# A hybrid decoder layer: blocks of L stored whole and read by a strided load, substitution started a unit earlier, results fetched by two queues

## The reference, cut to what matters

```python
lmat = jnp.where(strict, jnp.einsum('bnhid,bnhjd->bnhij', kb, k) * decay, 0.0)
tinv = lax.linalg.triangular_solve(eye + lmat, eye, left_side=True, lower=True, unit_diagonal=True)
u = jnp.einsum('bnhij,bnhje->bnhie', tinv, vb)
```

## Time and profile before

| | us |
|---|---|
| median of 3 runs | 1263.91 |
| the runs | 1258.98, 1263.91, 1264.14 |
| span of the profiled execution | 1257.6 |
| TensorE busy in it | 1100.3 (87%) |
| VectorE, ScalarE, GpSimd busy | 263.9, 234.4, 247.1 |
| mean granted clock of TensorE | 0.945 |

### The profile page before, as it was taken

One profiled execution on the slowest core, in us unless ns is written; L12 is line 12 of the kernel. 1 busy time (PEld: TensorE's weight loads), 2 busy tenths in 40 slices (PEclk: granted clock), 3 DMA queues, 4 the chain that ended last, 5 costly groups with the idle time before them and its releaser, 6 DMA issues.

```text
span 1257.6 us, 29984 instructions
## 1 busy us (share of the span) xinstructions
PE 1100.3 (87%) x12063; PEld 576.4 (46%) x12064; DVE 263.9 (21%) x750; ACT 234.4 (19%) x556; POOL 247.1 (20%) x510
## 2 busy tenths in 40 slices
PE   5899989997999769999679999997766699999984
PEld 4678766645444324444224444443222244444432
DVE  1044593764111101111001111110100011111113
ACT  2242314133111111111001121110100011111112
POOL 0041103102222112222112222221111122222220
PEclk9899988987999979999889999999888899999997
DMA  9945936699999999999999928999999999999996
GB/s 338 321 147 218 318 107 188 229 318 370 388 428 427 426 429 426 427 427 426 426 428 427 427 104 340 429 427 427 428 427 427 426 428 427 427 428 414 418 429 276
DMA packets 74704, 463.74 MB, mean 369 GB/s; under 512 B 11354, under 2 KB 27675, under 8 KB 49940
## 3 DMA queue, kind: packets, MB, share of 16 engines
q1 hardware_dynamic: 70364, 461.03, 89.6%
q10 hardware_dynamic: 4259, 1.49, 0.6%
HBM read 455.64 MB, written 6.95 MB: 368 GB/s over the span
## 4 chain that ended last, share of the span: by engine, by line
PE 66%; DMA 21%; SPq 5%; DVE 4%; issue 2%; ACT 1%; another core or an unknown queue 0%; ACTq 0%; DVEq 0%
PE psum L612 25%; PE psum L639 13%; DMA work<-in_w_down 7%; PE psum L570 5%; DMA weights<-in_w_down 4%; PE psum L937 4%; PE psum L588 4%; DMA weights<-in_w_gu 4%; PE psum L1187 2%; PE psum L622 2%; DMA weights<-in_w_ada 2%; DMA weights<-gate_mod_scratch 2%; PE psum L577 2%; SPq L834 2%; PE psum L584 1%
## 5 line engine op out<-in xcount | busy, mean ns | idle before, releaser
L612 PE MATMUL psum<-weights,work 128*32 128x512 f32 x3136 | 376.5, 626 | 82.2 <-DMA weights<-in_w_gu 70.0
L612 PEld LDWEIGHTS psum<-weights,work 128*32 128x32 f32 x3136 | 103.4, 113 | 325.8 <-issue 222.9
L2417 POOL TENSOR_SCALAR work<-work 128x128 f32<-128x128 f32 x159 | 123.9, 789 | 615.1 <-PE psum L630 615.1
L2263 DVE TENSOR_TENSOR work<-psum,work 128x256 f32<-128x256 f32 x53 | 22.5, 425 | 825.3 <-PE psum L622 825.3
L639 PE MATMUL psum<-weights,work 128*32 128x256 f32 x2944 | 171.3, 381 | 6.6 <-DMA weights<-in_w_down 6.5
L639 PEld LDWEIGHTS psum<-weights,work 128*32 128x32 f32 x2944 | 90.7, 110 | 71.7 <-DMA weights<-in_w_down 10.4
L1705 ACT COPY work<-psum 128x512 f32<-128x512 f32 x53 | 31.0, 586 | 485.9 <-PE psum L612 485.9
L937 PE MATMUL psum<-work,weights 128*128 128x288 f32 x320 | 81.1, 410 | 2.0 <-DVE weights L1824 2.0
L570 PE MATMUL psum<-work 128*32 128x256 f32 x1296 | 82.6, 388 | 0.0
L570 PEld LDWEIGHTS psum<-work 128*32 128x32 f32 x1296 | 45.1, 114 | 54.3 <-issue 37.6
L937 PEld LDWEIGHTS psum<-work,weights 128*128 128x128 f32 x320 | 60.0, 190 | 19.7 <-issue 4.1
(11 more groups left out here) (379 smaller groups left out, 956.1 us busy)
## 6 DMA issues: line engine op xcount, KB each, us to landing
weights<-in_w_gu SPq DMA_DIRECT2D x116, 2048.0 KB, 31.5
weights<-in_w_down SPq DMA_DIRECT2D x58, 2048.0 KB, 32.6
weights<-in_w_ada SPq DMA_DIRECT2D x12, 2048.0 KB, 13.6
work<-in_w_gu SPq DMA_DIRECT2D x12, 2048.0 KB, 30.3
weights<-in_w_in SPq DMA_DIRECT2D x6, 2048.0 KB, 13.1
work<-in_w_down SPq DMA_DIRECT2D x6, 2048.0 KB, 36.9
weights<-in_w_out SPq DMA_DIRECT2D x2, 2048.0 KB, 9.0
out<-weights SPq DMA_DIRECT2D x8, 512.0 KB, 8.4
```

What stands on the lines that cost most here:

```text
L612: last = mm(bank(GB)[SLOTS * n:SLOTS * n + SLOTS, :], xTm[:, k % 2, k // 2, :], gu[:, k % 2, 512 * n:512 * n + 512], start=k == 0, stop=k ...
L2417: ins = g.tensor_scalar(selG[:, c, :], iota_bd if c == 2 else iota, cur[:, 0, c:c + 1], cur[:, 1, c:c + 1], ALU.is_equal, ALU.mult)
```

## The change

L is stored whole. For each chunk one DMA writes [128, 6, 128] in runs of 512 B, where four wrote the diagonal blocks in runs of 128 B. The rows of a head lie `P` elements apart in DRAM; with a block pitch of 32 x 128 + 32 elements, one strided load fetches all 48 diagonal blocks. The two stores are issued behind unit 14 instead of eight behind unit 16, the load behind unit 15 instead of 17, and the last `l_matrix` runs behind unit 14. `solve` starts behind unit 16, and its pieces are spread anew. The store of T and U stands on SyncE ahead of the gate rows. The 16 loads of the results are split, chunk 0 on SyncE and chunk 1 on ScalarE behind unit 22. The levels run behind units 23 (first) and 24 (second) instead of 24 and 25, and the transposes of v move to make room.

```diff
--- before.py
+++ after.py
@@ -189,8 +189,9 @@
     gm_dram = nc.dram_tensor("gate_mod_scratch", (SEQS, 4, 4 * P), F32, kind="Internal").ap()
-    l_dram = nc.dram_tensor("l_blocks", (2, NBLK, H, SOLVE, SOLVE), F32, kind="Internal").ap()
-    t_dram = nc.dram_tensor("t_blocks", (2, NBLK, H, 2, SOLVE, SOLVE), F32, kind="Internal").ap()
+    BLK_PITCH = SOLVE * P + SOLVE
+    l_dram = nc.dram_tensor("l_blocks", (2, H, NBLK, BLK_PITCH), F32, kind="Internal").ap()
+    t_dram = nc.dram_tensor("t_blocks", (2, H, NBLK, 2, SOLVE, SOLVE), F32, kind="Internal").ap()
     ctx = ExitStack()
@@ -376,6 +377,15 @@
+        def t_block_loads(eng, c):
+
+            eng.wait_ge(s["blk"], 16 * BLK_STORED)
+            for k, dst in enumerate((Tm, Um)):
+                for r in range(NBLK):
+                    rows = slice(SOLVE * r, SOLVE * r + SOLVE)
+                    eng.dma_start(dst[c][rows, :, rows], t_dram[c, :, r, k].rearrange("h i j -> i h j")
+                                  ).then_inc(s["blk"], 16)
+
         ORDER = (2, 0, 1)
@@ -475,6 +485,7 @@
+        BLK_READ, BLK_STORED, BLK_LOADED = 3, 4, 4 + 4 * NBLK
         N_CONST, N_VEC, N_HIST, N_SMALL = 1, 5, 2, 20
@@ -692,6 +703,10 @@
             sp.dma_start(w_out_sb[1], w_out_half(1)).then_inc(s["wout_in"], 16)
+            sp.wait_ge(s["pooled"], 2)
+            sp.wait_ge(s["t0"], 2)
+            sp.dma_start(t_dram.rearrange("c h r k i j -> (c h r) (k i j)"), blk_tu[0:BLOCKS]).then_inc(s["blk"], 16)
+            t_block_loads(sp, 0)
             sp.wait_ge(s["modG"], 4)
@@ -699,16 +714,6 @@
             gate_rows(sp, 0, gm_tok, "gm_in")
-            sp.wait_ge(s["pooled"], 2)
-            sp.wait_ge(s["t0"], 2)
-            sp.dma_start(t_dram.rearrange("c r h k i j -> (c r h) (k i j)"), blk_tu[0:BLOCKS]).then_inc(s["blk"], 16)
-            sp.wait_ge(s["blk"], 16 * (2 * NBLK + 2))
-            for c in range(2):
-                for k, dst in enumerate((Tm, Um)):
-                    for r in range(NBLK):
-                        rows = slice(SOLVE * r, SOLVE * r + SOLVE)
-                        sp.dma_start(dst[c][rows, :, rows], t_dram[c, r, :, k].rearrange("h i j -> i h j")
-                                     ).then_inc(s["blk"], 16)
             sp.wait_ge(s["pool_ps"], 2)
@@ -1095,31 +1100,30 @@
                 if u == 23:
-                    pe.wait_ge(s["silu_done"], CT)
-                    pe.wait_ge(s["qkdT"], 2)
-                    to_tokens(3, PB)
                     pe.wait_ge(s["qkdT"], 3)
-                    to_tokens(4, PA)
-                if u == 24:
-                    pe.wait_ge(s["kv_tok"], 5)
-                    pe.wait_ge(s["blk"], 16 * (6 * NBLK + 2))
+                    pe.wait_ge(s["blk"], 16 * BLK_LOADED)
                     level_product(pe, mm, 1)
                     level_product(pe, mm, 2)
-                    pe.wait_ge(s["s_silu"], 3)
-                    pe.wait_ge(s["kv_tok"], 4)
-                    to_tokens(5, PB)
+                    pe.wait_ge(s["silu_done"], CT)
+                    to_tokens(3, PB)
+                    level_updates(pe, mm, 1)
+                    level_updates(pe, mm, 2)
+                if u == 24:
                     pe.wait_ge(s["u_sb"], 2)
...
                     tail_transposes(0)
-                    level_updates(pe, mm, 1)
-                    level_updates(pe, mm, 2)
-                if u == 25:
-                    tail_transposes(1)
+                    pe.wait_ge(s["kv_tok"], 4)
+                    to_tokens(4, PB)
                     level_product(pe, mm, 3)
                     level_product(pe, mm, 4)
-                    tail_transposes(2)
+                    tail_transposes(1)
                     level_updates(pe, mm, 3)
                     level_updates(pe, mm, 4)
+                if u == 25:
+                    pe.wait_ge(s["s_silu"], 3)
+                    pe.wait_ge(s["kv_tok"], 5)
+                    to_tokens(5, PB)
+                    tail_transposes(2)
                     tail_transposes(3)
@@ -1537,22 +1541,24 @@
                            ).then_inc(s["poolT"], 1)
+                if u == 14:
+                    for c in range(2):
+                        act.wait_ge(s["lmat"], c + 2)
+                        rows_of_head = l_dram[c].rearrange("h r x -> h (r x)")[:, 0:P * P]
+                        act.dma_start(rows_of_head.rearrange("h (p m) -> p h m", p=P), Lm[c]).then_inc(s["blk"], 16)
                 if u == 15:
+                    act.wait_ge(s["blk"], 16 * (BLK_READ - 1))
+                    blocks = l_dram.rearrange("c h r x -> (c h r) x")[:, 0:SOLVE * P]
+                    act.dma_start(blk_l[0:BLOCKS], blocks.rearrange("b (i m) -> b i m", i=SOLVE)[:, :, 0:SOLVE]
+                                  ).then_inc(s["blk"], 16)
                     act.wait_ge(s["rk2"], 1)
...
                     evacuate(0, None, Us, "u0_ps", "u0")
-                    act.wait_ge(s["lmat"], 3)
-                    for c in range(2):
-                        for r in range(NBLK):
-                            rows = slice(SOLVE * r, SOLVE * r + SOLVE)
-                            act.dma_start(l_dram[c, r].rearrange("h i j -> i h j"), Lm[c][rows, :, rows]).then_inc(s["blk"], 16)
                 if u == 17:
                     tokens(2, PA)
-                    act.wait_ge(s["blk"], 16 * 2 * NBLK)
-                    act.dma_start(blk_l[0:BLOCKS], l_dram.rearrange("c r h i j -> (c r h) i j")).then_inc(s["blk"], 16)
                 if u == 18:
@@ -1564,20 +1570,21 @@
                     evacuate(2, PA, QKT[1], "qkdT_ps", "qkdT")
+                    t_block_loads(act, 1)
                 if u == 23:
-                    tokens(3, PB)
-                    tokens(4, PA)
-                if u == 24:
                     first_factors(1)
                     first_factors(2)
-                    tokens(5, PB)
-                    tail_row(0)
+                    tokens(3, PB)
                     t_update(1)
                     t_update(2)
-                if u == 25:
-                    tail_row(1)
+                if u == 24:
+                    tail_row(0)
+                    tokens(4, PB)
                     first_factors(3)
                     first_factors(4)
+                    tail_row(1)
+                if u == 25:
+                    tokens(5, PB)
                     for q in range(2, 5):
@@ -1968,33 +1975,34 @@
                     l_matrix(1, PA)
-                if u == 15:
                     l_matrix(2, PB)
...
                     masked(0)
+                if u == 16:
+                    v.wait_ge(s["pooled"], 1)
+                    v.wait_ge(s["blk"], 16 * BLK_READ)
+                    solve(0, 6)
                 if u == 17:
                     value_scales()
-                    v.wait_ge(s["pooled"], 1)
-                    v.wait_ge(s["blk"], 16 * (2 * NBLK + 1))
-                    solve(0, 3)
+                    solve(6, 10)
                 if u == 18:
                     sample_conv(0)
-                    solve(3, 6)
+                    solve(10, 12)
                 if u == 19:
...
                     tt(Us[0:NS], Us[0:NS], prep_out(0, None), ALU.subtract).then_inc(s["tu_done"], 1)
-                    solve(6, 12)
+                    solve(12, 16)
                 if u == 20:
-                    solve(12, 16)
+                    solve(16, 19)
                     v.wait_ge(s["norm_ps"], 2)
...
                     qk_decayed(1, PB)
-                    solve(16, 26)
+                    solve(19, 25)
                 if u == 21:
                     qk_decayed(2, PA)
-                    solve(26, SOLVE - 1)
+                    solve(25, SOLVE - 1)
                 if u == 22:
@@ -2029,18 +2037,18 @@
                 decayed_keys(o)
+            u_update(1)
+            u_update(2)
             v.wait_ge(s["kv_tok"], 4)
...
             own(gate_weights(1))
+            u_update(3)
+            u_update(4)
             v.wait_ge(s["kv_tok"], 5)
             own(scale_values(2))
-            u_update(1)
-            u_update(2)
             v.wait_ge(s["kv_tok"], 6)
             own(scale_values(0))
-            u_update(3)
-            u_update(4)
@@ -2355,7 +2363,7 @@
             own(g.tensor_copy(seq_of, of_seq))
-            g.wait_ge(s["blk"], 16 * (2 * NBLK + 2))
+            g.wait_ge(s["blk"], 16 * BLK_STORED)
             g.wait_ge(s["s_silu"], 3)
...
```

## The result

The changed kernel is faster: median 1251.91 us of 21 runs against 1257.95 us of 21 runs of the kernel before, ratio 0.9942, 95% interval 0.9926 to 0.9958. That is 0.58%, 7.3 us (5.3 to 9.3). The forecast was 2.0 us, taken off a median of three runs, 1263.91: 1261.9, with 1256 as the low end of its range. The 21 runs put that median at 1257.95, so 6.0 of the 10.0 us between 1261.9 and 1251.91 are the base. The other 4.0 are the gain: 6.0 by the medians and 7.3 by the ratio, instead of 2.0. Rival 1 named a gain of that size: with the load at 137, "7.5 in all".

The account below looks back on a forecast made before the run. Bound: a dependence chain (L out and back, substitution, T back) beside a TensorE with nearly no slack. New_values starting 0.8 us earlier plus 1.2 at new_values gave 2.0 off the median 1263.91: 1261.9 us, range 1256 to 1269.

Parts of the forecast that it names:

- Rival 1: Block load slips past the weight loads, landing at 133 to 137; 1256.4 us at 137 (7.5 earlier); chance 0.20.
- the arrival of the blocks: Load of L's diagonal blocks: takes 12 us beside weight loads, landing at 141.5 instead of 147.6, some 6 us gained.
- the landing of the second store: Second store of L, ScalarE's queue: 768 turns against weight loads, 4.3 us, plus 1.74 and about 1; landed about 129.
- no such pause is likely now: Weight loads during the block load: running dry, as once at about 134.5 before, was held unlikely.
- the step with 38.4 us of VectorE work: VectorE from block landing to T: 36.4 us as before plus 1.5, 0.3 and 0.2; T ready at 179.9, not 184.1.
- TensorE before unit 23: Two stalls only moved, to a new 2.9 us at ada 10; 3.91 us one gone; unit 23 at 179.0, not 182.68.
- T back: Store and reload of T: store landed at 183.8, SyncE's loads at 189.4, ScalarE's, behind its evacuations, last at 191.3.
- The stall at the levels: TensorE behind unit 23, at first level products: wait of 0.72 us becomes 5.3 us, until the last block at 191.3.
- some 4 us: Sample-state loads, landing near 209, and GpSimd's masks: both hidden by some 4 us before they are needed in new_values.
- The clock and the rest: First products to new_values: 19.1 us work, 0.6 evacuations, 3.0 clock loss; gap inside unit 25 at 0; new_values 1.2 back.
- Rival 2: Behind the new stall after unit 23: half clock through unit 24, 6 to 6.7 us more, 1268 to 1268.6; chance 0.15.
- The sum: At new_values: 191.3 + 19.1 + 0.6 + 3.0 = 214.0 against 214.78, 0.8 earlier; with 1.2 at new_values, 2.0.

Follow-up runs that it names:

- e1: The changed kernel run again for a profile, beside the kernel before: 1251.25 us, ratio 0.9946 to the kernel before.
- e4: Changed kernel with the substitution's first ten columns behind unit 17 instead of six behind unit 16: 1251.34 us, ratio 0.9939 to the kernel before.
- e5: Changed kernel with level joins and transposes of v in their old order: 1250.01 us, ratio 0.9910 to the kernel before.
- e10: Kernel before plus only whole, early L and respread substitution (T store behind gate rows, 16 loads on SyncE, old levels): 1248.34 us, ratio 0.9921.
- e7: Changed kernel with the T store and SyncE's eight loads behind the gate rows again: 1253.14 us, ratio 0.9951 to the kernel before.
- E2: Changed kernel with all 16 result loads on SyncE, none on ScalarE: 1255.15 us, ratio 0.9959 to the kernel before.
- E8: Kernel before with only the levels and transposes of v in the new order: 1265.20 us, ratio 1.0040 to the kernel before.
- e3: Changed kernel with L in eight small stores at the new places and one contiguous load: 1248.93 us, ratio 0.9915 to the kernel before.
- e6: e5 with L in eight small stores and one contiguous load: 1247.03 us, ratio 0.9888 to the kernel before.
- e9: e6 with the gate rows behind the eight sample-state loads on SyncE: 1248.28 us, ratio 0.9905 to the kernel before.
- e12: e10 with L in eight small stores and one contiguous load: 1246.51 us, ratio 0.9919 to the kernel before.

## Why the prediction was wrong

**The step that failed** is the arrival of the blocks: "landed at about 129 ... I take 12 ... landed at 141.5", which is 19.4 us behind the mark. They landed 16.0 behind it in e1, and 16.0 to 17.8 in all seven runs with the strided load. Two terms were wrong. The first is the landing of the second store: it was given 768 turns against weight loads that had only just been issued. In e1 the weights' first packet came when more than half of the store had gone, and it landed 4.0 us behind the mark, not 6.9. Where it was issued 0.2 us later (e4, e5, e10) it lost that race and landed at 8.4, later than I had it, and still the blocks were early. So the second term weighs more: I had one pace for all of the load's packets and dismissed the pause in the weights, "no such pause is likely now". It came in 134 to 135, and let 632 packets through in e1; in e4 it was 1334 in 134 to 136. What was a turn lost to the store isn't lost to the load again, because by the traces the load ends in the pause wherever it starts; no run took the pause away.

That the load took 11.98 us in e1 for a forecast 12 is luck: 3.5 us without a packet, which the sum did not have, 5.5 us of turns, and then the pause. And rival 1 had the size, 7.5 us, partly by luck: the landing was 138 on the time base of before, not 137, and 1.3 us came from ScalarE, which it didn't have. The substitution began 3.4 us earlier than forecast, of which 3.1 went on to T (54.7 against 57.8), as the step with 38.4 us of VectorE work had it (38.6).

**TensorE before unit 23.** The forecast was 3.7 us earlier; it was 9.1. Two things are missing. The stalls of 2.03 and 1.86 us, "only moved" to ada 10 by my account, fell to 0.79 and 0.58 with the earlier load; with 1.48 at the last transposes, 4.9 of the 7.8 us went. And the two dips from 159.7 and 180 went with them: the rows of TensorE in them were 3.1 and 1.1 us longer before. I had priced a clock that a new stall loses and none that a removed one gives back. It brought little here. Unit 23 waited 1.48 us for VectorE in e1, and behind it TensorE stood at the blocks. In e7 the norms had the same stall of 0.6 us as in e1, the clock fell all the same, and unit 23 began at 51.6 against 51.5; 158.5 to 161.5, in e7 and in e1:

```profile
...
158.50:161.50 3.00, 3.00 (x46) 0.50 0.01 3
158.50:161.50 3.00, 3.00 (x48) 1.00 0.28 31
...
```

**T back.** Forecast 11.4 us from T to the last block, measured 10.1: ScalarE's issues don't wait for its copies. The trace of before had shown it, at 131.57, where its stores went out beside two copies. E2 confirms the worth of the second queue where TensorE stands at the blocks, 3 to 4 us; with the levels as before, 16 loads on SyncE cost only a stall of 0.51 us (e10).

**The stall at the levels.** Forecast 5.3, measured 6.27; right in kind. E8 shows its price by itself, 5.0 us, and e10 that the whole change is no faster than its one part without it. By the traces new_values starts 5.4 us earlier with the old order (e5); in that execution the wait for the sample states, of which the forecast said that they are hidden by "some 4 us", took all of it again.

**The clock and the rest.** From the first products to new_values 22.7 were forecast, with 3.0 for the clock, and 21.5 measured. Unit 24 lost 1.4 us, the products and transposes ahead of it about another 1.5. The gap inside unit 25 was taken at 0 and is absent in e1; the 1.2 us at new_values came back. Rival 2 is refuted: the clock was back at 1.00 at 194, within unit 24. The Trainium skill's rule ("TensorE: Matmul & The Clock Gate", Part 4: PE-mode transpose) that spoke for it is neither shown nor refuted here, as transposes and small products came together. But the dip at 207 of before doesn't speak for it as the prediction had it: e10 ran the same transposes and small products behind a gap of 1.92 us, and its clock was 1.00 throughout, in 198 to 208.

**The sum.** New_values at 91.9 from the mark was forecast (214.0), 86.4 measured: 5.5 us, of which 4.4 at the blocks (3.1 of the load, 1.3 of ScalarE) and 1.2 behind them. From there the shift did carry: 6.3 us at new_values, 7.0 at the first expert, 7.3 by the ratio.

**Stores whole or small.** The Trainium skill's rule on 512 B ("DMA: Bandwidth & Descriptors", Specifications) was read as a gain for the stores and a loss for the load. The loss is there: the strided load of 128 B runs took 8.2 to 12.2 us, the contiguous one 5.8 to 6.6 (e3, e6, e9, e12), though with fewer packets as well as longer runs, which no run tells apart. The gain of the stores is not shown: with whole stores the block load went out 3.6 us earlier where the second one got ahead of the weights (e1, e3), 0.4 later in e5 than in e6, and 0.7 earlier in e10 than in e12. E3 against e1 and e6 against e5 agree at 2.3 and 3.0 us in favour of the small ones.

## What to carry to other kernels

Two transfers on one crowded queue must be costed together, by the packets that both have to get through before the competing loads end; adding a worst case for each counts the same traffic twice. Look for a pause in the competing traffic above all: here it fixed the landing, wherever the transfer began. When a change takes stalls away from TensorE, look at the granted clock behind each as well, and then at what bounds next, since what the clock gives back can be lost there. And a part that opens a wait (here the levels moved ahead of their cover) should be tried apart from the part that earns: without it at least the same gain came with a smaller edit, and the next wait in line, the sample states, could be seen (e5, e6).

## What the runs showed of the hardware

The first packet of the two weight loads came between 1.1 us (e4) and 2.1 us (e1) behind the first one's issue, and the store that was issued 0.23 us ahead of that load in e1 and 0.03 us in e4 got through or met it: the next load was issued 4.0 or 8.4 us behind the mark, and 5.5 in e7, with 0.12 us. Beside the weights the strided load got one packet for one of theirs (662 and 663 in 4 us, of 128 B and 2 KB), and in the pause between two weight loads 632 in one microsecond. ScalarE issued DMAs (179.87) while copies that stand ahead of them in its program had not begun (180.13). And the idle time without a releaser inside unit 25 was 0.66 to 2.96 us in the versions with the old order of the levels and absent in the others. Why it comes is open: it was 0.66 and 1.00 us where the first state load had been issued 2.5 to 2.6 us ahead of it (e5, e6), and 1.73 to 2.96 where that was 5.7 to 5.8 us (before, e9, e10, e12). No run took away the burst of small products ahead of it.
